# One transfer of 2 MB for an expert's gate and up weights, in place of two halves

## The reference

```
group_prob = softmax(h @ w_group_router + group_bias)         # 4 groups, the best one
e_prob     = softmax(expert logits within that group)         # 4 experts each, the best two
gates      = g_prob * e_val, for 2 of the 16 experts
a = h @ w_e_gate[e];  u = h @ w_e_up[e]                       # [1024, 256] each
hid = silu(a) * u * gates
out = hid @ w_e_down[e]                                       # [256, 1024]
```

## Time and profile before

| | us |
|---|---|
| median of 3 runs | 2289.88 (2289.04 to 2290.8) |
| profiled execution, its own time | 2291.89 |
| its span, first to last instruction | 2290.1 |
| PE busy in it | 2078.8 (91%) |
| DVE busy | 1228.1 (54%) |
| ACT busy | 855.7 (37%) |
| POOL busy | 503.4 (22%) |
| gate/up transfers of the experts | 46, 1024 KB each |

### The profile page before, as it was taken

The page is one execution under the profiler, slowest core; times in us unless marked ns, Lnnn a source line. Parts: engine busy times, 40 slices in busy tenths (PEclk is TensorE's granted clock), DMA queues, the critical chain, the costliest instruction groups (busy, mean ns, idle before and its releaser), DMA issues. The chain is left out here.

```text
span 2290.1 us, 30304 instructions
## 1 busy us (share of the span) xinstructions
PE 2078.8 (91%) x11592; PEld 1764.3 (77%) x11592; DVE 1228.1 (54%) x2334; ACT 855.7 (37%) x1402; POOL 503.4 (22%) x343
## 2 busy tenths in 40 slices
PE   6888898899999999798989999998899988789994
PEld 6787777788888788786768888877887877777773
DVE  3676454544444447745454454458942232478885
ACT  4444433421222345343342222223234452257772
POOL 2654321000000146432110000005443335110001
PEclk9999988999999999898999999999899999799997
DMA  4111100412221111110132222206545522389995
GB/s 153 56 56 38 37 29 19 175 68 98 110 110 55 42 56 56 38 37 28 37 120 111 110 88 77 110 1 177 83 134 167 166 103 111 150 324 394 396 398 214
DMA packets 61627, 270.95 MB, mean 118 GB/s; under 512 B 15040, under 2 KB 19904, under 8 KB 37056
## 3 DMA queue, kind: packets, MB, share of 16 engines
q1 hardware_dynamic: 52864, 237.84, 30.0%
q10 hardware_dynamic: 6048, 22.02, 2.5%
q0 software_dynamic: 2592, 9.44, 1.1%
HBM read 244.14 MB, written 37.19 MB: 123 GB/s over the span
## 5 line engine op out<-in xcount | busy, mean ns | idle before, releaser
L1241 PE MATMUL fill_ps<-w_hi,h_hi 128*128 128x256 f32 (+1 forms) x704 | 214.0, 304 | 13.9 <-ACT values L866 5.2
L1241 PE MATMUL fill_ps<-w_hi,h_lo 128*128 128x256 f32 (+1 forms) x704 | 204.7, 291 | 0.0
L1241 PE MATMUL fill_ps<-w_lo,h_hi 128*128 128x256 f32 (+1 forms) x704 | 204.3, 290 | 0.0
L795 POOL TENSOR_TENSOR w_lo<-w_raw,w_hi 128x1024 fp32r<-128x1024 f32 x60 | 151.7, 2537 | 190.5 <-ACT w_hi L858 189.6
L516 DVE TENSOR_TENSOR ffn_silu<-ffn_silu,ffn_up 128x512 f32<-128x512 f32 x44 | 30.3, 688 | 285.2 <-ACT ffn_silu L474 285.2
L322 POOL TENSOR_SCALAR norm_ss<-norm_ss 128x1 f32<-128x1 f32 x24 | 4.9, 203 | 798.5 <-ACT ffn_raw_d L316 738.1
L1241 PEld LDWEIGHTS fill_ps<-w_hi,h_hi 128*128 128x128 f32 x704 | 141.6, 201 | 27.6 <-issue 16.7
L1702 POOL TENSOR_TENSOR w_lo<-w_raw,w_hi 128x1024 fp32r<-128x1024 f32 x48 | 125.1, 2622 | 166.4 <-ACT w_hi L1790 166.4
L528 DVE TENSOR_TENSOR x<-ffn_down,x 128x512 f32<-128x512 f32 x176 | 119.2, 689 | 71.1 <-PE ffn_down L590 70.3
L575 PE MATMUL ffn_up<-h_hi,w_hi 128*128 128x512 f32 x384 | 152.1, 396 | 3.7 <-PEq L772 3.7
L1321 PEld LDWEIGHTS o_ps<-values,prob_t 128*128 128x128 f32 x800 | 110.6, 200 | 57.1 <-DVE prob_t L1100 46.3
(11 more groups left out here) (444 smaller groups left out, 5644.4 us busy)
## 6 DMA issues: line engine op xcount, KB each, us to landing
moe_raw_gu<-in_w_e_gu SPq DMA_DIRECT2D x46, 1024.0 KB, 11.3
w_raw<-in_w_mix SPq DMA_DIRECT2D x28, 1024.0 KB, 4.9
w_raw<-in_w_two SPq DMA_DIRECT2D x23, 1024.0 KB, 4.9
moe_raw_d<-in_w_e_down SPq DMA_DIRECT2D x23, 1024.0 KB, 8.5
w_raw<-in_w_gate SPq DMA_DIRECT2D x22, 1024.0 KB, 5.1
w_raw<-in_w_up SPq DMA_DIRECT2D x22, 1024.0 KB, 6.5
ffn_raw_d<-in_w_down SPq DMA_DIRECT2D x22, 1024.0 KB, 4.9
moe_in<-in_zero SPq DMA_DIRECT2D x23, 512.0 KB, 7.7
```

Source lines behind the costliest of these rows:

```text
L795: nc.gpsimd.tensor_tensor(w_lo[s][:, cols], w_raw[s][:, cols], w_hi[s][:, cols].bitcast(F32), ALU.subtract).then_inc(lo_done, 1)
L1241: last = nc.tensor.matmul(b[:, 0:cols], aw[:, k, t * P:(t + 1) * P], ww[:, k, 0:cols], start=k == 0 and n == 0, stop=k == KD - 1 and n == 2)
```

## The change

The four semaphores of the halves become two, one for each buffer. `load_gu` transfers the whole buffer, 128 partitions x 16 KB, 2.097 MB. SP issues it when both halves of the buffer have been read by w_lo. Both w_hi of a block wait for the same semaphore, so the first too waits for all of the 2 MB. The conversions and the products themselves, their halves and their order stay as they are, as do the other transfers.

```diff
--- before.py
+++ after.py
@@ -2466,14 +2466,13 @@
         self.core, self.ctx = core, ctx
         self.gu = [core.sb("moe_raw_gu0", [P, KD, 2 * HID], ctx=ctx, side="right")]
         self.down = [core.sb("moe_raw_d0", [P, HB, D], ctx=ctx, side="right")]
-        self.gu_in = [[core.sem(f"moe_gu_in{s}{h}", ctx) for h in range(2)] for s in range(2)]
+        self.gu_in = [core.sem(f"moe_gu_in{s}", ctx) for s in range(2)]
         self.down_in = [core.sem(f"moe_d_in{s}", ctx) for s in range(2)]
-        self.sems = self.gu_in[0] + self.gu_in[1] + self.down_in
-
-    def load_gu(self, sp, e, s, h):
-        k0, k1 = h * KD // 2, (h + 1) * KD // 2
-        src = self.w["w_e_gu2"][e].rearrange("p (k n) -> p k n", k=KD)[:, k0:k1, :]
-        sp.dma_start(self.gu[s][:, k0:k1, :], src).then_inc(self.gu_in[s][h], 16)
+        self.sems = self.gu_in + self.down_in
+
+    def load_gu(self, sp, e, s):
+        src = self.w["w_e_gu2"][e].rearrange("p (k n) -> p k n", k=KD)
+        sp.dma_start(self.gu[s][:], src).then_inc(self.gu_in[s], 16)
 
     def load_down(self, sp, e, s):
         src = self.w["w_e_down2"][e].rearrange("p (k n) -> p k n", k=HB)
@@ -2481,8 +2480,7 @@
 
     def first(self, sp):
 
-        for h in range(2):
-            self.load_gu(sp, 0, 0, h)
+        self.load_gu(sp, 0, 0)
         self.load_down(sp, 0, 0)
 
     def second(self):
@@ -2490,8 +2488,7 @@
         self.down.append(self.core.sb("moe_raw_d1", [P, HB, D], ctx=self.ctx, side="right"))
 
     def ahead(self, sp):
-        for h in range(2):
-            self.load_gu(sp, 1, 1, h)
+        self.load_gu(sp, 1, 1)
         self.load_down(sp, 1, 1)
 
 
@@ -2694,9 +2691,8 @@
                 for b in range(2, BLOCKS):
                     s = b % 2
                     e = b if b < EXPERTS else spills[b - EXPERTS]
-                    for h in range(2):
-                        sp.wait_ge(gu_lo_done, 2 * (b - 2) + h + 1)
-                        w_moe.load_gu(sp, e, s, h)
+                    sp.wait_ge(gu_lo_done, 2 * (b - 2) + 2)
+                    w_moe.load_gu(sp, e, s)
                     sp.wait_ge(d_lo_done, b - 1)
                     w_moe.load_down(sp, e, s)
                 for s in range(2):
@@ -2727,7 +2723,7 @@
 
                 def w_hi(b, h):
                     s = b % 2
-                    act.wait_ge(gu_in[s][h], 16 * (b // 2 + 1))
+                    act.wait_ge(gu_in[s], 16 * (b // 2 + 1))
                     if b >= 2:
                         act.wait_ge(up_sum, b - 1)
                     nc.scalar.copy(gu_hi[s][:, h * HK:(h + 1) * HK, :],
```

## The result

| | before | after |
|---|---|---|
| median, us | 2290.34 (2289.04 to 2291.74, 4 runs) | 2308.88 (2306.98 to 2311.86, 4 runs) |
| span of the profiled execution | 2290.1 | 2307.0 |

The ratio on record is 1.0088, with a 95% interval of 1.0072 to 1.0103. It is an estimate from all of the runs, and the quotient of the two medians is a little lower, 1.0081: 18.5 us between the medians, 16.9 between the spans. 2297.5 was predicted, with a range of 2289 to 2307. The direction and the place were right, the size was not.

The account below looks back on a forecast made before the run. The prediction took the DMA engines to bound the expert blocks. Dry queue 4.5, drain 2.6 and start 0.5 summed to 7.6 us slower: 2297.5 us on the scale of the medians, range 2289 to 2307.

Parts of the forecast that it names:

- the range named: Sign in the expert blocks: DMA share falls to 0.96-0.99 with 385 to 392 GB/s, period rises to 10.6-10.9 us.
- The request: SP's next weight request in each block: leaves 9.05 us after the gate/up landing, where before it was 6.46.
- The second w_hi: Sign on ACT: a block's second w_hi never waits; ACT waits for gate/up some 17 times, once a block.
- The drain: After the last gate/up landing: w_hi and all behind it start later, 2.6 us slower (2.15 to 2.8).
- Bigger rows and one transfer for two: Gate/up loads: 16 KB rows for 8 KB and one SP issue fewer, value 0; at most 0.26 us a block.
- The first step: Expert blocks before the change: DMA engines set the pace, share 1.00 at 398 GB/s, 10.54 us a block.
- part 2: SP's queue in the expert blocks: cover shrinks from 4.0 to 1.4 us, 0.3 us lost a period, 4.5 us (0 to 15).
- The start term: Start of the experts: gu(2) asked for later, traffic put behind the scatter instead of ahead, 0.5 us (0 to 2.2).
- B (the queue never dry): SP's queue: cover of 1.4 us just holds, period stays, only drain and start remain: +3.1, 2293.0 us; chance 0.25.
- C (the x load becomes the wait): x loads behind 16 KB packets: up to 2.5 us more, 0.6 beyond slack, every period: 2302.6 us; chance 0.13.
- D (the boundary goes): Boundary between halves goes, queue stays full: 2288.3 or 2286.2 us, decided by a rate above about 405 GB/s; chance 0.12.

Follow-up runs that it names:

- e7: Kernel before, with SP asking for both gate/up halves only when the whole buffer is free; ACT still waits half by half: 2290.05 us, 1.0009.
- e1: Kernel before with its two 1 MB transfers; only the first conversion w_hi of a block waits for both halves: 2310.83 us, 1.0104.
- e3: Changed kernel, with SP asking for the next gate/up weights as soon as their buffer is free, ahead of the down weights: 2280.64 us, 0.9970.
- e4: Kernel before, with halves, SP asking for the next gate/up weights as soon as their buffer is free, ahead of the down weights: 2277.52 us, 0.9949.
- e8: Changed kernel, with SP's gate/up and down requests leaving at the same moment as there, but gate/up first: 2283.26 us, 0.9972.
- e2: Kernel before, with SP also waiting for x_lo before asking for the down weights and the next gate/up halves: 2293.96 us, 1.0025.
- e5: Kernel before, gate/up transfers cut at 1.5 and 0.5 MB, both asked for when all is free; first w_hi waits for 1.5 MB: 2302.77 us, 1.0057.
- e10: Changed kernel, with 12 unused transposes on PE ahead of its wait for h_lo in blocks 2 to 20: 2306.71 us, 1.0074.

## Why the prediction was wrong

**What held.** The share of 0.96 was in the range named (0.96 to 0.99), though not its rate (385 to 392 GB/s; 365 came) nor the period (10.6 to 10.9). Both requests leave together, and SP's merged wait costs nothing that can be told: e7 shows it by itself. The request moved to 8.99 us after a landing that ACT waited for, against 9.05 worked out. The second w_hi of the block shown doesn't wait, 2.07 us behind the first (2.16 said), though ACT waits for gate and up 8 times, not 17. The drain was 2.5 us against 2.6. Bigger rows and one transfer for two are worth nothing that can be told: e1 loses as much with the old transfers.

**The first step, that "the DMA engines set the pace", failed as a floor.** I read share 1.00 at 398 GB/s as full. e3, e4 and e8 move 414 to 420 GB/s in the same stretch at a share of 1.01 or 1.02. A share counts the time that packets take, and a packet that takes longer fills it as well. The packet records of the traces, 2074.00 to 2228.40, show it. Most packets of 8 KB take 309 to 311 ns and most of 4 KB 159, before the change, after it and in e4. In the kernel before, SP's queue was never without a packet under way (0.02 us in all), but its 8 KB packets took 327.6 ns in the mean, against 313.0 in e4. What all the packets took beyond 309 and 159 ns adds up to 8.1 us of the 16 engines' time before, and to 2.1 in e4. Before, nine tenths of what SP's queue has of it lie 2 to 6 us behind SP's requests, around the landing of the previous load. Why packets are slow there isn't shown.

So before the change the engines always had packets, and yet could carry more. How late or early the next weights come can be followed round a loop. SP's request waits for down_lo of two blocks before, hence for the landing that this block's w_hi waited for. The weights then wait in SP's queue behind 1 MB of down weights. Let D be the time from a landing of gate and up to the next block's load_down, and T the time from there to the landing of the gate and up weights asked for just behind it (in e8, just ahead of it), two blocks on. From the traces, means over 14 blocks (landings of 6 to 19 for D):

| | D | T | (D + T) / 2 |
|---|---|---|---|
| before | 6.54 | 14.58 | 10.56 |
| after | 9.51 | 13.49 | 11.50 |
| e8_order_only | 9.67 | 10.41 | 10.04 |

D + T is two periods by its definition, so the last column is only the period of the same blocks (10.56, 11.50, 10.04). What the table shows is where the period lengthens. It doesn't show by itself what limits it.

**The step that failed is the price of part 2: 4.5 us predicted (15 x 0.3), 15.7 measured (16 x 0.98).** By my own reckoning D grows by 2.6, and all but 0.6 (two periods of 0.3) comes back as a shorter T, since the queue had been covered for 4.0 us; T should have been near 12.6 (14.58 - 2.0). It was 13.49. D grew by 2.97 and T gave back only 1.09, so 1.88 stay in two periods. The bound of 1.0 a period was right at its edge, and the range of 2289 to 2307 was drawn to leave most of that very case out. The value of 0.3 came from one spell of 2 us, for which nothing said that its loss was typical. The larger part of T was never looked at: with the same requests and only their order reversed it is 10.41, 3.1 us less.

Two things in that reckoning can be named. First, I let the rate fall only with the share (385 to 392 GB/s at 0.96 to 0.99). SP's queue did run dry, as forecast: after the change it had no packet under way for 9.7 us of the 154.4, in 20 spells, 0.7 us a period. But the packets took longer as well: beyond their usual times (611 ns for one of 16 KB), 14.9 us in place of 8.1. By an estimate from these figures, 4% go with the lower share and 4% with the slower packets. Together they make the 8% between 398 and 365 GB/s. Second, I priced the hold on ACT, outside the drain, by the late request alone. By e2 the request alone is worth some 6 us, near the 4.5 predicted, though it leaves a little earlier there (D is 8.97 in the mean, against 9.51). The rest comes only when ACT itself is held.

**What I had not foreseen is PE's clock.** D and T hold a cost of compute. Ahead of five downs PE stood idle for 2.1 to 4.1 us, and these ran, at least in part, at a granted clock of 0.50. Idle time ahead of down, and its length to the end of its last product, for the downs that start between 2075 and 2240 after the change:

| start of down | idle before, us | length, us |
|---|---|---|
| 2077.1 | 2.90 | 4.56 |
| 2111.1 | 3.03 | 4.61 |
| 2146.2 | 4.06 | 5.49 |
| 2203.1 | 2.14 | 4.60 |
| 2226.8 | 2.46 | 4.61 |
| 2180.2 | 1.87 | 3.06 |
| the other blocks | up to 1.43 | 3.02 to 3.04 |

Five slow ones make 8.8 us over 3.02 each. In the kernel before, PE's longest wait there was 1.5 us and none was slow; in e3 it was 0.3. The Trainium skill (TensorE: Matmul & The Clock Gate, HAM oscillation — how this bites in real kernels) describes this pattern: a wait for a transfer in each round sends TensorE back to its slower clock, and the products behind it start slow. This trace agrees in five of 15 blocks. In the other ten the products ran at full speed. I did not weigh it, because the earlier trace rows showed a clock of 1.00 throughout the stretch; I should have asked which idle time the change would make longer.

It can feed back. x_turn follows down on PE, and the next x is asked for behind x_turn. After the slow down of the block shown, x was issued at 2082.55, 1.1 us behind SP's two requests, and landed at 2093.75, 11.2 us later; the median is 8.0.

**The start term (0.5) did not show.** POOL asked for the x of block 2 at 2020.53 against 2020.74, and block 6 landed 1.6 us earlier, not later. That landing lies between 2065.2 (e3) and 2076.0 (e5) in the ten profiled executions, 2074.07 before and 2068.92 in e1, so one execution of each kernel can't tell so small a term or its sign:

```profile
2020.53 1.16 POOL L2686 DMA_DIRECT2D moe_rows<-moe_in  x2 [9.97 <-DMA moe_in<-moe_rows,moe_slot]
```

**The rivals.** B (the queue never dry) falls with the share of 0.96 and the period of 11.43. C (the x load becomes the wait) came nearest in its time, 2302.6, but not by its mechanism: between 2060 and 2242 none of PE's waits names x, and 16 name moe_ht_lo. The rule beside it, of the Trainium skill (DMA: Bandwidth & Descriptors, Queues, rings and completion order), that an engine goes round its queues packet by packet, would have slowed x under 16 KB rows. Between the change (8.0 us median) and e1 with 8 KB rows (8.8) nothing of it is seen, but there the queue runs dry and the x loads scatter (4.2 to 12.8 us after the change). In e3 and e4, whose queue stays full and whose order is the same, the traces agree with it, as does e8 with 16 KB rows (9.7). The x loads from 2074.00 to 2228.40, in e3 and then in e4:

```profile
moe_rows<-moe_in ACTq DMA_DIRECT2D x14, 512.0 KB, 10.4
...
moe_rows<-moe_in ACTq DMA_DIRECT2D x14, 512.0 KB, 8.1
```

Each of e3's takes longer (9.8 at least) than any of e4's (9.2 at most): 2.3 us more, where C had up to 2.5. It costs no time there, as the periods of both are alike. D (the boundary goes) gained nothing. The 405 GB/s from which it was to decide are passed only where the requests are in the other order (e3, e4, e8), and e4, the fastest, still has the boundary between the halves. The fixed cost of a transfer that stands beside D (the Trainium skill, DMA: Bandwidth & Descriptors, Anatomy of one DMA) is given there for transfers that GpSimd issues, and these are SP's; no term of the sum went by it.

**What stays open.** How the 15.7 us split between waiting for weights and the slow clock; that the clock has a part in them is argued, not shown. The 8.8 us of slow products can't be set beside the waits as a term of their own: part of them may lie inside the next wait for weights. Nor did a run settle why T, with the queue nearly empty at the request, stayed 0.9 us above the reckoning. e10 removes the slow clock and its ratio is 0.0014 lower, within both intervals, with a filler that costs time itself. A kernel in which the clock stays up at no cost to PE was not tried. Nor is it explained why half of the hold (e5) costs two thirds of the loss, or why packets take longer around the end of a load when the next one was asked for late or stands behind the down weights.

## What to carry to other kernels

Ask for transfers in the order in which they are used: the order of two requests in one queue was worth 25 us here with the whole transfer (after against e8) and 10 with halves (before against e4), more than the size of the transfer or the time of the request. A DMA share of 1.00 is not proof of a bound; compare its GB/s with an undisturbed stretch, and look for a loop from a landing through the work to the next request. Before a wait is made coarser, add up what waits behind it, the next request among it, and ask what the longer gap does to TensorE's clock.

## What the runs showed of the hardware that was not expected

- The same DMA engines show a share of 1.00 at 398 GB/s before, and 1.02 at 420 in e4 with the same transfers in another order. The difference lies mostly in the packets: those of 8 KB took 327.6 ns in the mean against 313.0, where most take 309. In one stretch of 2 us they showed 1.11 at 442.
- In the stretch after the change TensorE was granted 0.50 of its clock behind idle gaps of 2.14 to 4.06 us ahead of down, and not behind gaps of 1.87 and less; twelve 128x512 products took 4.6 to 5.5 us in place of 3.02. The length of the gap alone does not decide it. At 2043.5, still in the start of the experts, a down behind 2.60 us ran at full speed in the kernel after, where in the kernel before, behind 2.58 us at 2043.7, it was slow (4.35). The same holds between other kernels: behind the gap in e8 (the first line) the twelve products took 3.03 us, behind the shorter one in e7 (the second), near the end of the experts, 4.61.

```profile
2076.81 0.50 PE L2948 MATMUL moe_down_ps<-moe_d_hi,moe_ht_hi 128*128 128x512 f32 x1 [2.35 <-DVE moe_ht_lo L2840]
...
2259.80 0.50 PE L2947 MATMUL moe_down_ps<-moe_d_hi,moe_ht_hi 128*128 128x512 f32 x1 [1.65 <-DVE moe_ht_lo L2839]
```

- With a full queue, 16 KB rows in SP's queue made the 4 KB rows of x in ACT's queue slower to come: 0.5 MB in 10.4 us (e3) against 8.1 with 8 KB rows (e4).
- One transfer of 2 MB gave no shorter period than two of 1 MB with the new order of requests (9.85 and 9.86). With the old order it was 11.43 against 11.87 in e1, in single profiled executions of kernels whose medians lie 2 us apart.
